# A decoder step on one core: samples' scores from keys turned on TensorE, prompt units inside the value projection, and the mixer's gates inside u with a split output projection

## The reference, cut to what matters

```
def mixer_a(h, w_in, v_norm, w_s, b_s, w_out):
    z = jax.nn.gelu(h @ w_in)
    u, v = jnp.split(z, 2, axis=-1)                 # 2048 features each
    v = rmsnorm(v, v_norm)
    gate = chunk_spatial_mix(v, w_s, b_s)           # mixes along 128 tokens, 8 groups of 256 features
    return (u * gate) @ w_out, v
# layer A: x += mixer_a(norm(x)); x += peer(norm(x))
# shared:  k, v = norm(x) @ w_kv                    # 12 heads of 64, in 3 groups of 4 heads
# layer B: x += attention(norm(x) @ w_q, k, v) @ w_o; x += peer(norm(x))
# prompt attention: group g sees keys at distance d*j, j = 0..128, d = 1, 4, 16
# sample attention: each sequence sees its own cache rows at the same distances, and its new keys
#   softmax runs over the three groups together (each output is weighted by its group's share)
```

## Time and profile before

| | |
|---|---|
| median of three runs | 2469.11 us (2466.82 to 2471.54) |
| the profiled execution's own time | 2469.67 us |
| its span | 2467.9 us, mean granted TensorE clock 0.977 |
| busy, share of the span | PE 96%, PEld 89%, DVE 66%, ACT 33%, POOL 2% |
| chain that ended last | PE 93%, DVE 3%, ACT 3%, issue 1% |
| DMA | 348.91 MB, mean 141 GB/s |

### The profile page before, as it was taken

The page is one execution under the profiler, slowest core; times in us unless marked ns, Lnnn a source line. Parts: engine busy times, 40 slices in busy tenths (PEclk is TensorE's granted clock), DMA queues, the critical chain, the costliest instruction groups (busy, mean ns, idle before and its releaser), DMA issues.

```text
span 2467.9 us, 47356 instructions
## 1 busy us (share of the span) xinstructions
PE 2371.3 (96%) x19442; PEld 2190.4 (89%) x19442; DVE 1620.8 (66%) x3502; ACT 817.4 (33%) x1080; POOL 43.0 (2%) x74
## 2 busy tenths in 40 slices
PE   7999999999999999999999799999999999999997
PEld 5888877989999999998976488779899999999996
DVE  5534599787756873875466266997787477648743
ACT  4502212342353244224201332123423432542332
POOL 1000000000000000000111000000000000000000
PEclk9999999999999999999998699999999999999998
DMA  5424343443444444444584043334344443454442
GB/s 200 171 96 148 120 136 119 137 136 133 140 162 152 147 153 156 153 136 139 187 251 138 1 142 117 135 118 138 135 137 139 168 154 137 154 170 137 136 154 70
DMA packets 51249, 348.91 MB, mean 141 GB/s; under 512 B 6112, under 2 KB 6128, under 8 KB 11408
## 3 DMA queue, kind: packets, MB, share of 16 engines
q1 hardware_dynamic: 44928, 324.16, 38.6%
q0 software_dynamic: 6192, 22.95, 3.0%
HBM read 342.83 MB, written 4.26 MB: 141 GB/s over the span
## 4 chain that ended last, share of the span: by engine, by line
PE 93%; DVE 3%; ACT 3%; issue 1%; DMA 0%; POOL 0%; DVEq 0%; ACTq 0%; POOLq 0%
PE ps L645 20%; PE ps L651 19%; PE ps L646 19%; PE ps L635 10%; PE ps L619 5%; PE ps L569 3%; PE ps L776 1%; PE ps L492 1%; PE ps L494 1%; PE ps L493 1%; ACT C_hi L1046 1%; PE ps L763 1%; PE ps L746 1%; PE ps L722 1%; PE ps L533 1%; PE ps L535 1%
## 5 line engine op out<-in xcount | busy, mean ns | idle before, releaser
L1456 DVE TENSOR_TENSOR w_lo<-ring,w_hi 128x1024 fp32r<-128x1024 f32 x448 | 544.4, 1222 | 267.3 <-ACT w_hi L1036 260.5
L1036 ACT ACTIVATE w_hi<-ring 128x1024 fp32r<-128x1024 f32 x448 | 473.1, 1057 | 635.9 <-PE ps L646 635.8
L645 PE MATMUL ps<-C_hi,w_hi 128*128 128x288 f32 x2048 | 630.3, 308 | 20.8 <-DVE C_lo L1511 20.3
L651 PE MATMUL ps<-C_hi,w_lo 128*128 128x288 f32 x2048 | 606.6, 296 | 0.0
L646 PE MATMUL ps<-C_lo,w_hi 128*128 128x288 f32 x2048 | 600.9, 293 | 0.0
L645 PE MATMUL ps<-h_hi,w_hi 128*128 128x288 f32 x1536 | 461.6, 301 | 3.3 <-DVE slots L1464 3.3
L646 PE MATMUL ps<-h_lo,w_hi 128*128 128x288 f32 x1536 | 454.8, 296 | 0.0
L651 PE MATMUL ps<-h_hi,w_lo 128*128 128x288 f32 x1536 | 453.4, 295 | 0.0
L645 PEld LDWEIGHTS ps<-C_hi,w_hi 128*128 128x128 f32 x2048 | 386.0, 188 | 26.5 <-DVE C_lo L1511 19.9
L646 PEld LDWEIGHTS ps<-C_lo,w_hi 128*128 128x128 f32 x2048 | 389.7, 190 | 0.0
L651 PEld LDWEIGHTS ps<-C_hi,w_lo 128*128 128x128 f32 x2048 | 386.6, 189 | 0.0
(11 more groups left out here) (245 smaller groups left out, 2501.9 us busy)
## 6 DMA issues: line engine op xcount, KB each, us to landing
ring<-in_U SPq DMA_DIRECT2D x128, 1024.0 KB, 4.8
ring<-in_V SPq DMA_DIRECT2D x128, 1024.0 KB, 4.9
ring<-in_peer_q SPq DMA_DIRECT2D x16, 1024.0 KB, 4.8
ring<-in_w_in_v SPq DMA_DIRECT2D x8, 1024.0 KB, 6.3
ring<-in_w_in_u SPq DMA_DIRECT2D x8, 1024.0 KB, 5.0
ring<-in_w_out SPq DMA_DIRECT2D x8, 1024.0 KB, 4.8
big<-in_cache POOLq DMA_DIRECT2D x16, 512.0 KB, 7.2
big<-in_cache POOLq DMA_DIRECT2D x16, 256.0 KB, 8.4
```

Source lines behind the costliest of these rows:

```text
L645: one = pe.matmul(out, w_hi[:, h % HI_SLOTS, at], hi, start=start, stop=False)
L651: return pe.matmul(out, w_lo[:, h % (2 * R), at], hi, start=False, stop=stop)
L1036: act.activation(w_hi[:, k % HI_SLOTS, :], ring[:, bl % R, (k % 2) * HBLK:(k % 2 + 1) * HBLK], ACT.Copy).then_inc(hi_made, 1)
L1456: dve.tensor_tensor(w_lo[:, n % (2 * R), :], ring[:, n // 2 % R, n % 2 * HBLK:(n % 2 + 1) * HBLK], w_hi[:, n % HI_SLOTS, :], ALU.subtract) ...
```

## The change

Mixer. u is no longer a loop of its own: `mixer_u` makes the gate of chunk h - 7 behind u's chunk h, so that 8 of 16 gates stand inside u, one more behind it by the same line, and seven follow. VectorE gates a chunk as soon as it is there and ScalarE has made its u. ScalarE then writes the upper part of u*gate (`ug_hi`), VectorE the lower in place (`ug_lo`), and the output projection becomes a split stage with three fp32r products per block. Its weights are halved by ScalarE and VectorE like the others' (numbers 32 to 47 of the early halves), and the next stage's first three halves are made at chunks 5, 6 and 7, the third behind the last chunk.

Attention. The keys of a sequence are loaded as before in three groups, those of the third group over all 128 partitions (4 loads instead of 3). Five sequences are loaded when three quarters of the first peer's V stage are done, the other three behind the clearing of `Qz`, `Qd` and `zeros` by GpSimd at the peer's end. TensorE turns each sequence's keys (`turn_keys`, 14 transposes in 4 banks), ScalarE copies them to `KT` (two places), and TensorE multiplies them with that sequence's queries (`key_products`, six f32 products of 64 stationary columns, two heads' queries beside zeros in `Qz`). All 8 sequences add up in banks 6 and 7, so the scores come out as queries by keys. The first two turnings stand inside the query projection, the others behind each key chunk. VectorE copies the projected keys. The softmax mask of group 2 and 3 comes from `tmask`.

The units' scores and turnings now stand inside the value projection (scores of unit n + 1 and turning of unit n - 1 behind value product n, the samples' probabilities behind the fourth); the turned probabilities of all units are kept. Behind it come the samples' value products in one block (32 output partitions each), and then the units' products. The 24 small copies are VectorE's.

```
+GATE_LAG = 7
+            def mixer_u():
+                for h in range(16):
+                    pe.wait_ge(elo_made, 16 + h + 1)
...
+                    three.then_inc(act_full, 1)
+                    if h == GATE_LAG:
+                        pe.wait_ge(v_ready, 1)
...
+                    if h >= GATE_LAG:
+                        mixer_gate(h - GATE_LAG)
...
+            mixer_u()
+            for c in range(16 - GATE_LAG, FC):
+                mixer_gate(c)
             for c in range(DC):
-                r = arrived(state["block"])
                 b = dve_bank("wo", c)
-                for f in range(FC):
-                    last = pe.matmul(ps[:, b, 0:T], ring[:, r, f * P:(f + 1) * P], uT[:, f, :],
-                                     start=(f == 0), stop=(f == FC - 1))
+                for n in range(2 * c, 2 * c + 2):
+                    pe.wait_ge(elo_made, 32 + n + 1)
+                    for k in range(8):
+                        f = n % 2 * 8 + k
+                        if c == 0:
+                            pe.wait_ge(ug_lo_made, f + 1)
...
+                        one = pe.matmul(out, ew_hi[:, n % HI_SLOTS, at], ug_hi[:, f, :], start=(f == 0), stop=False)
+                        two = pe.matmul(out, ew_hi[:, n % HI_SLOTS, at], ug_lo[:, f, :], start=False, stop=False)
+                        last = pe.matmul(out, w_lo[:, n % (2 * R), at], ug_hi[:, f, :], start=False, stop=(f == FC - 1))
...
+            for k in range(HI_LEAD + 5, 16):
+                early_lower(16, k)
+                gated(k - HI_LEAD - 5)
+            for c in range(16 - HI_LEAD - 5, FC):
+                early = c - (16 - HI_LEAD - 5)
+                if early < HI_LEAD:
+                    early_lower(32, early)
+                gated(c)
+                gated_low(early)
+            for c in range(8, FC):
+                gated_low(c)
+            early_lower(32, HI_LEAD)
...
+            pool.wait_ge(dve_free, D0["V0"] + 3 * DC)
+            for b in range(5):
+                load_cache(b, 0, k_landed[b])
+            pool.wait_ge(x_ready, 2)
+            pool.memset(Qz, 0.0).then_inc(queries_cleared, 1)
...
+            def turn_keys(b):
+                pe.wait_ge(k_landed[b], 16 * 4)
+                for j in range(4):
+                    bank = act_bank("kt", 4 * b + j)
...
+                    for k, at in enumerate(pieces):
+                        last = pe.transpose(ps[:, bank, k * P:(k + 1) * P], Kc[:, b, at:at + P], ident[:])
+                    last.then_inc(act_full, 1)
+            def key_products(b):
+                pe.wait_ge(act_free, A0["kt"] + 4 * (b + 1))
...
+                for g in (1, 2, 0):
+                    n = CK[g] * CS[g]
+                    for c in range(2):
+                        dst = ps[c * 64:c * 64 + 64, 6, 0:512] if g == 1 else (
+                            ps[c * 64:c * 64 + 64, 7, SC_AT[g] - 512:SC_AT[g] - 512 + n])
+                        last = pe.matmul(dst, Qz[:, 2 * g + c, 64 * b:64 * b + 64],
+                                         KT[:, b % 2, KT_AT[g] + c * n:KT_AT[g] + (c + 1) * n],
+                                         start=(b == 0 and g == 1), stop=(b == NB - 1), skip_group_check=True)
...
                     last.then_inc(dve_full, 1)
+                    key_products(n)
+                    turn_keys(n + 2)
...
                     last.then_inc(values_full, 1)
+                    if n == 3:
+                        turn_samples()
+                    if n:
+                        turn_unit(n - 1)
+                    if n + 1 < 8:
+                        prompt_scores(n + 1)
...
+            pe.wait_ge(turned_free, TURNED[7])
+            pe.wait_ge(vc_loaded, 16 * 4 * NB)
```

More of the change, by code:

```diff
@@ new lines, in prompt_scores @@
+            def prompt_scores(u):
+                h, m = u // 2, u % 2
+                row = (h % 2) * HD
+                n = P * (m + 1)
+                for g in range(NG):
+                    if g == 0 and u:
+                        pe.wait_ge(dve_free, D0["ps"] + 3 * (u - 1))
+                    bank, at = (4, g * P) if m == 0 else (5 + g // 2, g % 2 * 256)
+                    pe.matmul(ps[:, bank, at:at + n], aq[row:row + HD, 2 * g + h // 2, m * P:(m + 1) * P],
+                              ak[row:row + HD, 2 * g + h // 2, 0:n], start=True, stop=True).then_inc(dve_full, 1)
@@ L857, in _ @@
-            pe.wait_ge(act_free, A0["pp"])
-            pe.wait_ge(vc_loaded, 16 * NG * NB)
-            sample = sample_products()
-            nsample = sum(2 + NB * s for s in CS)
-            def sample_share(k):
-                last = None
-                for _ in range(share(k, 12, nsample), share(k + 1, 12, nsample)):
-                    last = next(sample)
-                return last
-            def unit_bank(kk):
-                if kk >= 2:
-                    pe.wait_ge(act_free, A0["pp"] + kk - 1)
-                return kk % 2
@@ L1158, in _, with turned_bank @@
[L1158 to L1165 removed]
+            turned = {"n": 0}
+            def turned_bank():
+                turned["n"] += 1
+                act.wait_ge(turned_full, turned["n"])
+                return 2 + (turned["n"] - 1) % 2
@@ L1166, in _ @@
+            act.wait_ge(samples_full, 1)
+            for k, bank in enumerate((2, 3, 7)):
+                last = act.activation(sampled[:, 2 * k:2 * k + 2, :].rearrange("p a b -> p (a b)"), ps[:, bank, :], ACT.Copy)
+            last.then_inc(samples_moved, 1)
             for u in range(8):
@@ L1284, in add_chunks @@
                 for c in range(DC):
+                    if stage == "wo":
+                        for k in range(4 + 2 * c, min(6 + 2 * c, 16)):
+                            early_lower(32, k)
                     b = full(stage, c)
@@ L1587, in _ @@
[L1587 to L1595 removed]
+            for n in range(AC):
+                dve.wait_ge(dve_full, D0["k"] + n + 1)
+                dve.tensor_copy(ak[:, n, :], ps[:, 4 + n % 2, 0:T]).then_inc(dve_free, 1)
@@ L1608, in unit_scores @@
                 if u >= 2:
-                    dve.wait_ge(act_free, A0["pp"] + sum(3 if w % 2 else 2 for w in range(u - 1)))
-                full("ps", 3 * u + 2)
+                    dve.wait_ge(turned_free, TURNED[u - 2])
+                dve.wait_ge(dve_full, D0["ps"] + 3 * u + 3)
                 for g in range(NG):
```

617 lines of the change are left out of this document (304 added, 313 removed).

## The result

The changed kernel takes 2415.15 us (median of four runs, 2412.68 to 2417.17), the kernel before 2468.29 beside it: ratio 0.978 (95% interval 0.9766 to 0.9795). It is 53 us faster. The profiled execution took 2412.68 us (span 2410.9, mean granted clock 0.990), 57.0 less than that of before.

What follows compares the result with a forecast made beforehand. TensorE was taken as the bound, busy 96% of the span, slow at the mixer's end and in attention. Mixer 7.3 plus attention 28.9 made 36.2 us off 2469.67, 2433.5, forecast as 2433 from the runs' median; range 2418 to 2451.

Steps and rivals of the forecast that it cites:

- the samples' tail: Attention's end: samples' value products 19.2 us, units' products 13.0, samples' transposes 2.4, last copy 0.7.
- Attention, TensorE's queue added up: Attention: TensorE's work without waits 159.3 us, waits 4.1, clock 3; sum 166.4 against 195.3, 28.9 won.
- the term for the clock: Attention, key stage and samples' probabilities: 3 us lost to a lower clock, bounds 0 and 12.
- TensorE comes to it out of 45 us of dense work: Argument for the rival that the attention's tail stays at full clock: 9.2 us less, 2424, chance 0.13.
- rival 2: Attention's keys and sample products: every change of tile shape costs 0.27 us, 5.4 in all, 2439; chance 0.10.
- The two halves of the array run beside each other: Attention's key products: pairs on two output halves overlap, 1.5 us per sequence instead of 3.0, 12.1 in all.
- The key step: Attention's key stage: one step takes 7.5 to 8 us; above 10 us would make the prediction wrong.
- rivals 1 and 6: Key stage: 1, halves don't run beside each other, 2445, chance 0.12; 6, clock falls and stays down, 2485, chance 0.05.
- 1.0 given back: Stage after the mixer: an upper half ahead of ScalarE's squares delays their sum, losing 1.0 us of the mixer's gain.
- The mixer: Gates inside u and split output projection: 8.3 us won, 1.0 given back, 7.3 net, bounds 3 and 12.
- The first output chunk: Mixer's output projection: first chunk follows VectorE's last subtractions and ends 0.4 us later, at 165.3.
- the 2.5 that I put for the clock: Mixer's output stage: 2.5 us lost to the clock behind a stretch of half-used TensorE, bounds 0 and 5.

Runs made afterwards that it cites:

- by_quarter: Changed kernel with the samples' value products reordered, all of one sequence (one quarter of the output columns) behind each other; 2445.34 us.
- scores: Changed kernel with 24 added products of 64 x 128 by 256 columns ahead of the samples' value products, no added pause; 2427.9 us.
- gap_scores: Changed kernel with an added TensorE wait of some 3 us, then 24 added products of 64 x 128, ahead of the samples' value products; 2441.31 us.

## Why the prediction was wrong, point by point

**The step that failed** is the samples' tail in "Attention, TensorE's queue added up", its terms for the samples' value products and the units, with the term for the clock. I took 0.12 for a sample row, between 0.092 "at full clock" and 0.136 at half, and 0.18 for a unit row, between 0.127 and 0.235: in both a clock near half. It was full. Measured against forecast: the sample products 10.25 against 19.2 (9.0 too much); units, turning and the last copy 10.9 against 13.0 + 2.4 + 0.7 = 16.1 (5.2); the clock loss 0 against 3, though at the samples' probabilities six other traces do show one, of 1.7. That is 17.2 of the 21.0 by which the attention beat the forecast. By the terms of my sum, 12.2 of it is the clock (4.5 in the sample rows, 3.9 in the units, 0.8 in the turning, 3 for the loss), and 5.0 is the size of the terms at full clock (14.7 against 10.25 in the samples' products, 11.4 against 10.9 behind them). The rest lies in stages whose mechanism I had right: queries 26.8 against 27.6, keys 47.7 against 49.7, values 49.7 against 50.8.

Why I took the half clock: I read the earlier trace rows, busy at 0.50, as the doing of small products. The row doesn't say that. It stands behind a wait of 1.74 us and is made in part of products of 64 rows, and the runs above show a long half clock only where the two come together. The change removed both from the tail, but for waits of 0.4 to 0.7 us: the scores moved into the value projection, where whole-array products surround them, and the third window's values now fill 128 rows. For that I had only the line that "TensorE comes to it out of 45 us of dense work", and gave it 0.13, at 2424. That sum leaves out the 3 us of clock loss that the rival's own sentence takes away; with it the rival stands at 2421.

Why even that rival was short: 3.9 us of it are the queries, keys and values, and 4.5 the samples' products, whose bound of 0.092 a row had been read from six rows in 0.55 us. A change of the array's shape is in these six, 0.13 to 0.14 by the runs of 8, 16 and 32 rows above. And six rows are three products, which fill at most three of the four quarters: one product alone takes 0.55 in `by_quarter`, and four take 0.57 in the changed kernel. Runs of different length give 0.054 a row. The Trainium skill has a rule on this (TensorEngine Tiling (Array Packing), Tiling Modes): a change of tiling mode empties TensorE first. The twelve changes inside the samples' block agree with it, at 0.13 to 0.14 us each. I had applied it as rival 2's extra price, at 0.27 a change, and not seen that the row I took my bound from held one.

**What was right.** The two halves of the array run beside each other: 1.66 us against 1.5 taken. The key step took 7.22 us, 7.5 to 8 forecast, at full clock. So rivals 1 and 6 are out, and rival 2's price was twice too high. u's end came at 145.9 against 145.8, and an output chunk takes 6.4. The mean square's wait is 1.2 instead of 0.26, 1.0 given back.

**The mixer** was forecast at 7.3. The last add came 7.6 earlier than before (8.3 forecast), less that 1.0; the part alone measured 0.23%, 5.7 us (3.0 to 8.4). That 7.6 is so near 8.3 is luck in part. The first output chunk was to end at 165.3, behind the last subtraction; it ended at 168.3, because TensorE's first output product waited for the sixteenth gate until 160.2. And the 2.5 that I put for the clock behind it did not come: it was 1.00 from 163.6 on. Of 6.9 at the first V add, 5.2 to 5.9 were left where the attention starts, because the last V stage ran at 12.80 a chunk instead of 12.66. That was not in the prediction, and its cause is open.

## What to carry to other kernels

A half clock in a busy stretch is a thing to be explained, not a price of the products in it: look for the last wait ahead of it and for what ran behind, and ask whether the change removes one of the two. A price taken from a short run of rows holds the change of shape on both sides; take it from two runs of different length, or subtract the change. And where one engine's chain stands behind another's stage, put as much of it inside as the other can hide: with the other half of the gates inside u, the mixer's last add came another 6.0 us earlier (207.37 against 213.32). And where one stage's clock is 1.00 in one execution and falls in another, read it in several traces before a part of the change is charged with it.

## What the runs showed of the hardware

- The same products ran at either level of the clock, by what stood ahead of them. 24 products of 64 x 128 kept 1.00 when they found it (`scores`) and ran at 0.50 behind a pause of 3.6 us (`gap_scores`); TensorE then ran without a pause for 34 us at 0.50 (1342 to 1376). The Trainium skill (TensorE: Matmul & The Clock Gate, Part 1) tells the clock by how busy TensorE has been; by the busy time of these rows in the profile, which is full, it would have come back, so here the measurement decides.
- Without products of 64 rows the clock was back 3.6 to 7.5 us behind a pause of 3.3 to 3.6 us, whether the products behind it had 64 columns, 32 (128 and 32 rows in turn), or one quarter at a time.
- A wait of 0.88 and 0.26 us in the value projection was followed by 3.5 us at 0.50 in six of fifteen traces, and by 1.00 in nine.
- f32 sample rows of 256 columns in four column quarters take 0.054 us each, with 16 or 32 output columns used alike. Each run, with its change between 128 and 32 rows, adds 0.13 to 0.14 us, and going out to the whole array and back in the middle of a run 0.29.
- The same stage of 96 fp32r products per chunk took 12.48, 12.66 or 12.80 us a chunk, at full clock and without a wait; what sets the level is open.
